# Norm sums one unit later in TensorE's order, and one rotation of three PSUM banks for norm sums and score tiles

## What is computed

```python
h = rms_norm(x, norm_gain)
parts = split(einsum("ntd,de->nte", h, w_in), SPLIT_POINTS)
# for each of 3 dilated groups (mixer A) and for the sliding window (mixer B):
q = rms_norm(heads(parts[...]), qk_norm[..., 0])       # per head, 64 wide
k = rms_norm(heads(parts[...]), qk_norm[..., 1])
v = heads(parts[...])
o, lse = banded_attention(q, k, v, slopes, sinks, window // dil, dil)
# merge
wts = softmax(lse_a, axis=0)
a = sum_g(wts * o_a) * silu(z_a)
b = o_b * silu(z_b)
mixed = sigmoid(g_a) * (a @ w_branch_a) + sigmoid(g_b) * (b @ w_branch_b)
y = x + mixed @ w_out
```

## Time and profile before

| | us |
|---|---|
| median of 3 runs | 2309.11 (2306.69 to 2353.67) |
| the profiled execution | 2317.27, span of its slowest core 2315.7 |
| spans of the 8 cores | 2283.2 to 2315.7 |
| busy: PE, DVE, ACT, POOL | 1887.8 (82%), 1258.6 (54%), 1226.0 (53%), 428.7 (19%) |
| norm sums on PE | 257, 99.1 us busy |
| the chain that ended last | PE 56%, ACT 14%, DMA 13%, issue 9%, DVE 6% |

### The profile page before, as it was taken

One profiled execution on the slowest core, in us unless ns is written; L12 is line 12 of the kernel. 1 busy time (PEld: TensorE's weight loads), 2 busy tenths in 40 slices (PEclk: granted clock), 3 DMA queues, 4 the chain that ended last, 5 costly groups with the idle time before them and its releaser, 6 DMA issues.

```text
span 2315.7 us, 43826 instructions; the slowest of 8 cores (2283.2 to 2315.7 us)
## 1 busy us (share of the span) xinstructions
PE 1887.8 (82%) x14352; PEld 1073.0 (46%) x14352; DVE 1258.6 (54%) x1948; ACT 1226.0 (53%) x2190; POOL 428.7 (19%) x519
## 2 busy tenths in 40 slices
PE   3676576798698987988889887785786999999995
PEld 1453453464455544555555544342333445444442
DVE  3454254545355553554545545664565677776773
ACT  3544365577476864767657766775787311111110
POOL 0122001112112130121311212321222111111110
PEclk8798778899899998999999998887898999999997
DMA  7498753599757896659964696779455568777764
GB/s 171 130 227 198 141 163 104 146 185 183 170 143 166 177 181 163 167 139 203 181 160 153 163 193 128 155 152 164 124 132 136 171 189 232 218 214 199 200 174 128
DMA packets 133998, 389.20 MB, mean 168 GB/s; under 512 B 15488, under 2 KB 87696, under 8 KB 129520
## 3 DMA queue, kind: packets, MB, share of 16 engines
q10 hardware_dynamic: 5680, 178.06, 33.4%
q1 hardware_dynamic: 97024, 119.95, 19.3%
q0 software_dynamic: 31072, 88.39, 18.6%
HBM read 363.23 MB, written 230.06 MB: 256 GB/s over the span
## 4 chain that ended last, share of the span: by engine, by line
PE 56%; ACT 14%; DMA 13%; issue 9%; DVE 6%; ACTq 1%; POOL 1%; DVEq 0%; SPq 0%; POOLq 0%
PE ps L53 56%; ACT nl L53 6%; DMA xT<-scr_x 4%; DMA rw<-win 3%; ACT expt L53 2%; DMA sa<-ra 2%; ACT sq L53 2%; ACT ld L53 1%; ACT rb L53 1%; DVE tt L53 1%; DVE rd L53 1%; DVE pt L53 1%; DVE ra L53 1%; DMA ld<-x 1%; DVE rb L53 1%
## 5 line engine op out<-in xcount | busy, mean ns | idle before, releaser
L53 PE MATMUL ps<-xT,rw 128*128 128x512 bf16 x2496 | 672.9, 406 | 27.8 <-DMA xT<-scr_x 21.4
L53 DVE TENSOR_TENSOR pt<-expt,mask 128x512 bf16<-128x512 f32 x512 | 388.7, 772 | 273.8 <-ACT expt L53 249.8
L53 ACT ACTIVATE expt<-ps 128x512 f32<-128x512 f32 x576 | 334.3, 595 | 156.1 <-PE ps L53 117.0
L53 PEld LDWEIGHTS ps<-xT,rw 128*128 128x128 bf16 x2496 | 252.9, 106 | 286.1 <-issue 87.2
L53 PE MATMUL ps<-ra,rd 64*128 64x128 bf16 (+2 forms) x1792 | 281.2, 280 | 93.3 <-ACT expt L53 52.6
L53 ACT ACTIVATE sq<-ps 128x512 bf16<-128x512 f32 x257 | 149.3, 581 | 237.5 <-PE ps L53 237.2
L53 ACT ACTIVATE nl<-ps,epsS 128x512 f32<-128x512 f32 x257 | 174.9, 680 | 154.4 <-PE ps L53 150.1
L53 PE MATMUL ps<-rw,xT 128*128 128x128 bf16 x3328 | 228.9, 228 | 28.5 <-DMA rw<-win 15.9
L53 PEld LDWEIGHTS ps<-ra,rd 64*128 64x128 bf16 (+1 forms) x1792 | 127.8, 102 | 267.2 <-issue 202.6
L53 PEld LDWEIGHTS ps<-rw,xT 128*128 128x128 bf16 x3328 | 217.3, 122 | 36.9 <-issue 30.2
L53 ACT ACTIVATE nl<-nl 128x512 f32<-128x512 f32 (+1 forms) x321 | 200.8, 626 | 29.8
(11 more groups left out here) (134 smaller groups left out, 2212.3 us busy)
## 6 DMA issues: line engine op xcount, KB each, us to landing
xT<-scr_x SPq DMA_DIRECT2D x40, 1024.0 KB, 10.9
sa<-ca ACTq DMA_DIRECT2D x32, 1020.0 KB, 10.1
ra<-ca POOLq DMA_DIRECT2D x48, 512.0 KB, 6.9
rw<-win POOLq DMA_DIRECT2D x78, 256.0 KB, 14.8
rb<-x SPq DMA_DIRECT2D x32, 512.0 KB, 6.2
rb<-xh SPq DMA_DIRECT2D x16, 512.0 KB, 8.8
scr_x<-xT POOLq DMA_DIRECT2D x8, 1024.0 KB, 10.0
scr_ab<-ra SPq DMA_DIRECT2D x64, 128.0 KB, 4.8
```

The lines of the kernel that those rows point to most:

```text
L53: return lambda eng: getattr(eng, name)(*args, **kwargs)
```

## The change

Norm sums are called one unit later: after the second PE step of the unit after next (`run_dfr` at `n == 1`, with the lists `dfr`, `dfr_old`, `dfr2`), no longer after the sixth step of the next unit. Entries without PE steps no longer call them early, except after `n_job`. Tiles are due one index later (`after = len(M) + 2` in all three places), since q and k are ready later. Norm sums lose their own bank 3: `rST` now hands out 3, 4, 5 in turn to norm sums, score tiles and transposes alike. The merge keeps banks 4 and 5 (`rMG`), the decode sums bank 3.

```diff
-    rPJ = Rot([0, 1, 2]); NB = 3; rST = Rot([4, 5]); UA, UB = 6, 7
+    rPJ = Rot([0, 1, 2]); rST = Rot([3, 4, 5]); rMG = Rot([4, 5]); UA, UB = 6, 7
...
-            si, ni, b0 = st_["si"], rNL.next(), bank[0]
+            si, ni, b0, NB = st_["si"], rNL.next(), bank[0], rST.next()
...
-            after = len(M) + 1
+            after = len(M) + 2
...
-                ba[half] = rST.next()
+                ba[half] = rMG.next()
...
-    SQB, PU = 2, NB
+    SQB, PU = 2, 3
...
-    dfr, dfr2 = [], []
+    dfr, dfr_old, dfr2 = [], [], []
+
+    def run_dfr():
+        for f, f2 in dfr_old:
+            f()
+            if f2 is not None:
+                dfr2.append([1, f2])
+        del dfr_old[:]
+
...
         for n, p in enumerate(u.pe):
             p()
-            if n == 5:
-                for f in dfr:
-                    f()
+            if n == 1:
+                run_dfr()
+        if u.post is not None:
+            if not u.pe and i > n_job and dfr_old + dfr:
+                dfr_old += dfr
                 dfr = []
-        if u.post is not None:
-            if not u.pe and dfr:
-                for f in dfr:
-                    f()
-                dfr = []
+                run_dfr()
             u.post()
+        if u.pe:
+            dfr_old, dfr = dfr_old + dfr, []
+            for item in list(dfr2):
+                item[0] -= 1
+                if item[0] < 0:
+                    item[1]()
+                    dfr2.remove(item)
         if u.dfr is not None:
-            dfr.append(u.dfr)
...
+            dfr.append((u.dfr, u.dfr2))
```

More of the change, by code:

```diff
@@ L1459, in build_program @@
             p()
-            if n == 5:
-                for f in dfr:
-                    f()
-                dfr = []
-        if u.post is not None:
-            if not u.pe and dfr:
-                for f in dfr:
-                    f()
-                dfr = []
-            u.post()
-        if u.dfr is not None:
-            dfr.append(u.dfr)
[L1472 to L1477, removed]
+            if n == 1:
[3 more added lines that the diff above has]
+                dfr_old += dfr
+                dfr = []
+                run_dfr()
+            u.post()
+        if u.pe:
[5 more added lines that the diff above has]
+                    dfr2.remove(item)
+        if u.dfr is not None:
+            dfr.append((u.dfr, u.dfr2))
         if u.bulkw:
```

## The result

The change makes the kernel slower: 2352.71 us median of 4 runs (2344.96 to 2356.98) against 2306.7 us for the kernel before, measured with it (three runs, 2297.68 to 2309.11). The ratio is 1.0205, 95% interval 1.0157 to 1.0254: the loss is clear of the noise, and whether it is more or less than 2% is not. So the sign and the range of the prediction hold, and the size does not: +46 us where +82 was forecast.

What follows compares the result with a forecast made beforehand. Mixer A was taken to hang on PE with little slack, B on a loop between ACT and PE. 2317.3 + 58 (A) + 24 (B) = 2399, less 8 to the median: 2391 us, range 2300 to 2470.

Steps and rivals of the forecast that it cites:

- What is late next: Three projection banks: unit i+3 cannot start less than 3.3 us after unit i+2, as unit i's bank is held.
- under 15: Sign of being right: PE's wait for the ACT square falls from 83 us to under 15.
- The size of A: Mixer A, 463 to 1405 us: 51 + 15 - 8 = +58 us, bounds -15 and +140.
- the 51 us of short intervals: Mixer A: 78 of 158 norm-unit intervals are below 3.25 us; what they lack to 3.32 us adds 51 us.
- The late places of ACT: Mixer A: where denominators make ACT late, 27 places give +29 and -14, so +15 replaces -41.6 us.
- The third score bank in A: Mixer A: three shared banks save a third of the exponentials' wait, -8 us, bounds 0 and -23.9.
- B: +24: Mixer B: windows grow to 42 us; eight at +4 would be +32, taken as +24 us, bounds -33 and +50.
- rival 3: The clock falls too: PE's idling costs 38 us in B and 32 us in A, 2461 us; 17%.
- Rotating banks: Skill rule: independent matmul groups rotate through different PSUM banks; by it alone the exponentials' waits go and time falls.
- Start: 0: Start, 0 to 463 us: the 34.8 us on the square go, the loop binds; 0, bounds -35 and +15.
- Last stage: 0: Gates, merge and output from 1800 us on: only bank names change, the 516 us stay.
- Rival 1: Waits change places: loop costs 51 us, 41.6 on the square and 8 of the exponentials' go, 2310 us; 20%.

Runs made afterwards that it cites:

- the late place with four banks: The changed kernel with four projection banks (0 to 3), norm sums and score tiles sharing banks 4 and 5: 2291.01 us, one run, no ratio.
- Rotation alone: The kernel before with banks 3, 4, 5 rotating for norm sums, score tiles and transposes, sums at their old place: 2290.85 us, ratio 0.9855.
- the three other versions of the first two groups: Changed kernel with sums in their own bank (1.0138); changed kernel with four projection banks (2291.01 us); four projection banks with sums at the old place (0.9954).

## Why the prediction was right, and where its sizes were off

**What is late next: right.** The step said that the bank of unit i, wanted by unit i+3, would bind, with a floor of 3.3 us. The shortest interval is 3.31, half of all are within half a us of it, and with the sum four matmuls later the floor moves by just these four matmuls, to 4.17. The wait for the square is gone where "under 15" was said, and waits for the multiplies are far over 100 us. A fourth bank takes all but 4 of the 47 us away.

**The size of A: near, because two errors partly cancel.** The prediction's stages were cut by time: its start, 0 to 463 us, holds A's first block and a bit more, and its A, from 463 us on, is about A's rest. I had +58 us there; it is +49 by the table and +43 on core 3. In the account of waits of A's rest on core 3, the waits for DVE that come were 51 + 41.6 + 15 = 108 us by my sum and are 137 (156.8, where 19.9 stood before). The waits that vanish were 50 by my sum (the square and 8 of the exponentials) and are 102: the square 43.6 by this cut, exponentials 22.9, and a part that I had not seen at all, loads of `xT` and `rw` 26.0 and ACT writing `rb` 9.7. The balance is 35 us, as much as the idle time rose (133.7 to 169.0); PE's busy time rose by 7. So the net came nearer than its two parts, by luck. That a slower loop gives the loads time fits the late place with four banks: its A is 62 us faster and its wait on `xT` is back, 32.4 us. The step that failed is the belief that the 51 us of short intervals "hold almost no wait that could go away": they hold none, but their neighbours do, and a stage that takes 50 us longer pays back waits that have nothing to do with the sums.

**The late places of ACT.** The step gave +15 us for late denominators. No run isolates them; if they are there, they sit in the longer intervals (a quarter are above 4.46 us). Open.

**The third score bank in A: -8 forecast, +2 found.** Rotation alone left A's rest at 985.2 against 983.2 us, which can't be told from -8. But it is not that a third of the exponentials' wait went: three quarters of it went, and the square and the loads took its place, as told above.

**B: +24 was wrong, it is +1.** Two terms were missed, and of opposite sign. With the rotation, the late place costs 18 us in B (301.2 to 319.3), which is near the 24; undisturbed windows now start at V units 1642.24, 1682.89, 1722.92 and 1762.12, so they take 40.6, 40.0 and 39.2 us against 38.4 and 37.9, and not 42. Measured from rotation alone, where the last two windows take 36.4 and 35.9 us, this is the +4 of the step, from a lower start. The rotation gives 17 us, where the step said "in B nothing, because there ACT is what is waited for". The stretch of B in rotation alone, on core 3, shows where they come from:

```profile
1389.40:1690.50 301.10, 226.71 (x1562) 112.69 (x1561) 191.64 (x310) 228.85 (x393) 83.56 (x75) 0.93 0.76 156
```

Against the same row of the kernel before above, PE is busy 14.9 us less for the same 1562 matmuls, at a granted clock of 0.93 instead of 0.87, and idle 5.4 us less. The waits for the exponential in B are 9.6 us in place of 36.2; those for the square (5.0 before) and for `ra` (23.9 before) have grown:

```profile
PE ps L53 <- DVE ra L53: 29.0, 6, 23.3
PE ps L53 <- ACT sq L53: 14.3, 18, 2.1
PE ps L53 <- ACT expt L53: 9.6, 14, 1.3
```

So three quarters of the gain is clock. The spacing of the matmuls says the same: of 418 neighbouring 128x512 matmuls in B, 78 start 0.427 us apart instead of 0.216 in the kernel before, and 30 in rotation alone. Over all cores, B's granted clock has a median of 0.92 in rotation alone and 0.87 to 0.89 before, after, and in the three other versions of the first two groups: the late place loses what the rotation had won. Every other version with the rotation in B and the sum after the fourth or the sixth step has 0.91 to 0.93 there. This is rival 3 with its sign turned. The clock did matter, in B, but the kernel before was already paying for it. The Trainium skill ("TensorE: Matmul & The Clock Gate", A second HAM failure mode: psum-queue depth-cycling) describes such swings when PE idles briefly between groups; that the clock is higher in the version whose longest wait for the exponential is 1.3 us and not 2.9 agrees with it. That the shorter waits are the cause is not shown: no run changes the waits and nothing else.

**The clock in A: rival 3 did not come.** With 143 us of waits for norm multiplies spread over 114 places the granted clock stayed at 0.94. With the sum four matmuls later it was 0.92.

**Rotating banks.** The rule of the Trainium skill ("Perfetto Trace Analysis", Matmuls) that independent groups rotate through different banks was set against this change's hold of the projection banks. The rotation by itself does bring 1.5%, so the rule agrees with that run; the whole change, which has the same rotation, is 2% slower. The hold of the projection banks makes the difference.

**Start: 0 was wrong by 18 us**, 8 in the start and 10 in A's first block. In the start the early calls at entries without PE steps are the likely part; the first block stays open. I had counted only the waits on the square and the loop.

**Last stage: 0 was said, and it is +9 us on core 3** (576.8 to 586.1), +5 by the median of the eight cores (576.3 to 581.8). PE's busy time there rose by 6.6 us at a clock of 0.94 against 0.95; what changed it was not looked for.

**Rival 1** named the right process, waits that vanish and pay the loop back. Of 137 us of new waits they paid 102, and only 66 of these were the square's and the exponentials'.

## What to carry to other kernels

When a dependent operation is moved later in an engine's order, write down which buffer it holds open, who wants that buffer next, and how long the chain from the moved operation to the buffer's release takes: place plus chain is a floor for the whole loop, and here it came to 0.01 us from the rows of the kernel before. Weigh it against the number of buffers, not against the wait that the move takes away; with one bank more the same move cost too little to be told from nothing. A floor that slows a stage also hides other lateness (loads here), so its price is less than the waits that it makes, here 35 us of idle time for 137 us of new waits. And two halves of a change with opposite signs need to be tried apart.

## What the runs showed of the hardware that I had not expected

In B, a third bank for score tiles changed the granted clock from 0.87 to 0.93 and PE's busy time by 15 of 242 us, while the idle time fell by 5 us only. In A, the clock stayed at 0.94 under 114 waits of 1.3 us on average, and was 0.92, worth some 20 of 893 us of busy time, when the loop's floor grew to 4.17 us a unit.
